# First attention layer in two groups of heads, with its projections, softmax and output projection interleaved

## The reference, cut to what matters

```python
def mla_mixer(h, cos, sin, w_down, q_a_norm, kv_a_norm, w_uq, w_ukv, q_norm, k_norm, w_o):
    down = h @ w_down                                    # 384 + 256 + 64 columns
    c_q = rmsnorm(down[..., :384], q_a_norm)
    c_kv = rmsnorm(down[..., 384:640], kv_a_norm)
    k_rope = down[..., 640:]
    q = (c_q @ w_uq).reshape(1, 256, 8, 192)             # per head 128 plain + 64 rotary
    kv = (c_kv @ w_ukv).reshape(1, 256, 8, 256)          # per head 128 key + 128 value
    k_nope, v = kv[..., :128], kv[..., 128:]
    k = concatenate([k_nope, broadcast(k_rope)], -1)
    q, k = rmsnorm(q, q_norm), rmsnorm(k, k_norm)        # over the head's 192 columns
    # rotary embedding on the last 64 columns of q and of k
    for blk in range(2):                                 # 128 queries at a time
        scores = einsum('bqhd,bkhd->bhqk', q[:, blk], k[:, :end]) * 192 ** -0.5
        p = softmax(where(causal, scores, -inf))
        outs.append(einsum('bhqk,bkhd->bqhd', p, v[:, :end]))
    return o @ w_o                                       # 1024 x 1024
```

## Time and profile before

| | us |
|---|---|
| median of three runs | 1415.55 |
| lowest and highest of them | 1414.0 to 1416.23 |
| the profiled execution, its own time | 1413.8 |
| its span from first to last instruction | 1411.8 |
| PE, DVE, ACT busy in the span | 1323.1, 1049.4, 864.3 |

### The profile page before, as it was taken

How to read it: one execution, slowest core, us unless ns; L and a number is a source line. 1 busy time by engine, 2 the same in 40 slices (tenths; PEclk the granted TensorE clock), 3 DMA queues, 4 the chain that set the end, 5 groups by cost and what they waited for, 6 DMA issues and landing times.

```text
span 1411.8 us, 18829 instructions
## 1 busy us (share of the span) xinstructions
PE 1323.1 (94%) x6088; PEld 1080.8 (77%) x6088; DVE 1049.4 (74%) x1488; ACT 864.3 (61%) x1274; POOL 38.8 (3%) x54
## 2 busy tenths in 40 slices
PE   7999999997687899999999999999997985999998
PEld 5878888886566788888888888888886753888887
DVE  4576555565755799999999999999995846555554
ACT  4655444456533587878787887878784544454443
POOL 0000000000300000000000000000000211000000
PEclk9999999998887999999999999999998977999999
DMA  9645545554013397979898999889894400355540
GB/s 356 217 143 207 179 179 191 195 178 150 1 60 120 147 383 296 383 299 377 316 367 330 340 342 337 338 338 371 325 375 134 179 30 1 119 182 195 188 150 30
DMA packets 46121, 319.30 MB, mean 226 GB/s; under 512 B 5152, under 2 KB 6304, under 8 KB 7808
## 3 DMA queue, kind: packets, MB, share of 16 engines
q1 hardware_dynamic: 44288, 316.39, 59.7%
q10 hardware_dynamic: 1680, 2.10, 0.5%
q0 software_dynamic: 112, 0.26, 0.1%
HBM read 316.64 MB, written 2.10 MB: 226 GB/s over the span
## 4 chain that ended last, share of the span: by engine, by line
PE 84%; DVE 9%; issue 3%; ACT 3%; DMA 1%; DVEq 0%; POOL 0%; SPq 0%; ACTq 0%; POOLq 0%
PE bank L350 24%; PE bank L352 24%; PE bank L351 24%; PE bank L641 2%; PE bank L414 2%; DVE wl L1223 2%; DVE x L1637 1%; PE bank L744 1%; PE bank L386 1%; DMA fixed<-fixed_dram 1%; PE bank L660 1%; PE bank L661 1%; PE bank L765 1%; PE bank L581 0%; PE bank L803 0%
## 5 line engine op out<-in xcount | busy, mean ns | idle before, releaser
L1223 DVE TENSOR_TENSOR wl<-raw,wh 128x1024 fp32r<-128x1024 f32 x598 | 714.8, 1221 | 208.5 <-ACT wh L828 197.7
L828 ACT ACTIVATE wh<-raw 128x1024 fp32r<-128x1024 f32 x598 | 631.4, 1061 | 327.3 <-PE bank L352 320.6
L350 PE MATMUL bank<-wh,xth 128*128 128x512 f32 (+2 forms) x1170 | 464.1, 397 | 15.0 <-DVE wl L1223 4.7
L352 PE MATMUL bank<-wh,xtl 128*128 128x512 f32 (+2 forms) x1170 | 455.4, 389 | 0.0
L351 PE MATMUL bank<-wl,xth 128*128 128x512 f32 (+2 forms) x1170 | 455.1, 389 | 0.0
L350 PEld LDWEIGHTS bank<-wh,xth 128*128 128x128 f32 x1170 | 221.8, 190 | 61.2 <-issue 7.7
L352 PEld LDWEIGHTS bank<-wh,xtl 128*128 128x128 f32 x1170 | 221.4, 189 | 46.2
L351 PEld LDWEIGHTS bank<-wl,xth 128*128 128x128 f32 x1170 | 222.2, 190 | 42.3
L350 PE MATMUL bank<-wh,hth 128*128 128x512 f32 x456 | 178.5, 391 | 0.0
L352 PE MATMUL bank<-wh,htl 128*128 128x512 f32 x456 | 177.9, 390 | 0.0
L351 PE MATMUL bank<-wl,hth 128*128 128x512 f32 x456 | 177.4, 389 | 0.0
(11 more groups left out here) (281 smaller groups left out, 853.5 us busy)
## 6 DMA issues: line engine op xcount, KB each, us to landing
raw<-weights_dram SPq DMA_DIRECT2D x299, 1024.0 KB, 4.9
x<-x_dram SPq DMA_DIRECT2D x1, 1024.0 KB, 7.7
bias_scratch<-act ACTq DMA_DIRECT2D x1, 1024.0 KB, 15.7
wide<-bias_scratch ACTq DMA_DIRECT2D x8, 128.0 KB, 2.6
out_dram<-x SPq DMA_DIRECT2D x4, 256.0 KB, 2.1
fixed<-fixed_dram SPq DMA_DIRECT2D x1, 596.0 KB, 8.8
rows<-rows_dram POOLq DMA_DIRECT2D x1, 256.0 KB, 6.1
cols<-cols_dram SPq DMA_DIRECT2D x1, 73.0 KB, 8.5
```

The source lines that it names most:

```text
L350: mm(o, lh, wh[:, wi, sl], start=start, stop=False)
L352: return mm(o, ll, wh[:, wi, sl], start=False, stop=stop)
L828: A(wh[:, c % SPLIT, :], raw[:, (c // 2) % RAW, (c % 2) * UNIT:(c % 2 + 1) * UNIT], ACT.Copy).then_inc(hi_done, 1)
L1223: V.tensor_tensor(wl[:, c % SPLIT, :], raw[:, (c // 2) % RAW, (c % 2) * UNIT:(c % 2 + 1) * UNIT], f32(wh[:, c % SPLIT, :]), ALU.subtract). ...
```

## The change

The stage's weights are stored in another order: units `R0` (rotary columns of all queries), `KA`, `QA0`, `VA` (keys, queries, values of heads 0 to 3), `KB`, `QB0`, `VB` (the same of heads 4 to 7), and the output projection by pairs of heads (`WO_UNITS`). Three units that are half empty are split over 512 columns only (`HALVED`). The latent rows are turned before their norm is known, the first eight transposes between the two last products of the down projection; the norm's factors enter later as scalars. The masked maximum of a head is made in one DVE operation for each of the two query blocks (`row_max`, a tensor-tensor-reduce with an accumulator), in place of four operations. The values are scaled on their copy out of PSUM, the keys straight from PSUM.

The order on PE (`c` and unit names as above):

```diff
+            pe.wait_ge(sem("qkT_d"), 1)
+            turn_k_rope(0, bank[6])
+            pe.wait_ge(sem("qkT_a"), 3)
+            pe.wait_ge(sem("qkT_d"), 3)
+            scores(0)
+            scores(1)
+            pe.wait_ge(sem("v_c"), 2)
+            product(QB0, 0, (0, 1), WIDE, bank[2:4], 0, 2)
+            turn_p(0)
+            scores(2)
+            product(QB0 + 1, 0, (2,), WIDE, bank[2:4], 0, 2)
+            values(0)
+            turn_p(1)
+            scores(3)
+            pe.wait_ge(sem("k_ready"), 2)
+            kv_chunk(VB, bank[0:2])
+            values(1)
+            turn_p(2)
...
+            scores(4)
+            scores(5)
+            wo(0)
+            turn_p(4)
+            scores(6)
+            wo(1)
+            values(4)
+            turn_p(5)
+            scores(7)
+            wo(2)
+            values(5)
+            turn_p(6)
+            wo(3)
+            values(6)
+            turn_p(7)
+            wo(4)
+            values(7)
+            wo(5)
+            wo(6)
+            turn_half("ffn1", 0, 4)
+            wo(7)
```

On DVE:

```diff
+            def row_max(h):
+
+                b = h % 2
+                dv.wait_ge(sem("head_S"), h + 1)
+                if h >= 2:
+                    dv.wait_ge(sem("head_PT"), h - 1)
+                for qb, (a, n) in enumerate(((0, P), (P, 2 * P))):
+                    c = 8 * (h // 4) + 4 * qb + h % 4
+                    r = V.tensor_tensor_reduce(out=ebuf[:, b, a:a + n], in0=bank[4 + b][:, a:a + n], in1=maskt[:, a:a + n],
+                                               scale=rs[:, c:c + 1], scalar=3.0e38, op0=ALU.add, op1=ALU.min,
+                                               accum_out=stat[:, 2 * b + qb:2 * b + qb + 1])
...
+            follow(KB, 1, 0)
+            q_scales(0)
+            evac_turned(4, 2048, bank[5], "kn")
+            evac_turned(6, 5120, bank[6])
+            row_max(0)
             k_sums(1)
...
+            follow(QB0, 1, 0)
+            row_max(1)
+            weigh(0)
+            k_scaled(1, bank[0:2])
+            follow(QB0 + 1, 1, 0)
+            row_max(2)
+            weigh(1)
+            out_lo(0)
+            q_sums(1)
+            follow(VB, 1, 0)
+            row_max(3)
+            weigh(2)
+            out_lo(1)
...
+            row_max(4)
+            row_max(5)
+            weigh(4)
+            follow(U_WO, 1, 0)
+            row_max(6)
+            out_lo(4)
+            follow(U_WO + 1, 1, 0)
+            weigh(5)
+            row_max(7)
+            out_lo(5)
+            follow(U_WO + 2, 1, 0)
+            weigh(6)
+            follow(U_WO + 3, 1, 0)
+            out_lo(6)
+            weigh(7)
+            out_lo(7)
+            follow(U_WO + 4, 1, 0)
```

On ACT in the output projection:

```diff
+            exps(4)
+            exps(5)
+            copy_p(4)
+            follow(U_WO, 1, 0)
+            exps(6)
+            out_hi(4)
+            follow(U_WO + 1, 1, 0)
+            copy_p(5)
+            exps(7)
+            out_hi(5)
+            follow(U_WO + 2, 1, 0)
```

More of the change, by code:

```diff
@@ L63 @@
 U_UQ = U_DOWN + 6
-U_UKV = U_UQ + 6
-U_WO = U_UKV + 4
+U_WO = U_UQ + 10
 U_MOE = U_WO + 8
@@ L561, in _ @@
[L561 to L570, removed]
+            product(U_DOWN + 4, 0, range(0, 4), 192, (bank[5], bank[7]), 0, KD - 1)
@@ L583, in _ @@
+            turn_q(1, 1, bank[0])
+            turn_k(1, 0, bank[1])
+            pe.wait_ge(sem("qkT_a"), 4)
+            turn_k(1, 1, bank[2])
+            pe.wait_ge(sem("qkT_d"), 4)
+            turn_k_rope(1, bank[3])
+            values(3)
             pe.wait_ge(sem("qkT_a"), 6)
             pe.wait_ge(sem("qkT_d"), 6)
[L585 to L612, removed]
-                        .then_inc(sem("head_O"), 1)
@@ L1005, in scale_q, with evac_q @@
-            def scale_q(heads):
-                for h in heads:
-                    for t in range(NT):
-                        A(qv[:, t, h, 0:NOPE], qv[:, t, h, 0:NOPE], ACT.Copy, scale=rs[:, 8 * t + h:8 * t + h + 1])\
-                            .then_inc(sem("q_ready"), 1)
-            for n in range(7):
-                if n < 3:
-                    follow(U_UQ + 2 * n, 2, 0)
+            def evac_q(half, banks):
+                for t in range(NT):
+                    A(act[:, t, 512 * half:512 * (half + 1)], banks[t][:, :], ACT.Copy).then_inc(sem("qn_c"), 1)
@@ new lines, in evac_v, with evac_turned @@
+            def evac_v(half, banks):
+                sc.wait_ge(sem("lora_rs"), 1)
+                for t in range(NT):
+                    A(act[:, t, 2560 + 512 * half:2560 + 512 * (half + 1)], banks[t][:, :], ACT.Copy,
+                      scale=rs[:, 50 + t:51 + t]).then_inc(sem("v_c"), 1)
+            def evac_turned(lot, at, o, gain=None):
+                sc.wait_ge(sem("qk_T"), lot)
+                g = {"scale": col(gain)} if gain else {}
+                A(wide[:, at:at + WIDE], o[:, :], ACT.Copy, **g).then_inc(sem("qkT_a"), 1)
@@ new lines, in out_hi @@
+            def out_hi(h):
+                sc.wait_ge(sem("head_O"), h + 1)
+                A(xth[:, oslot(h), :], bank[7][:, (h % 2) * 256:(h % 2 + 1) * 256], ACT.Copy).then_inc(sem("head_oh"), 1)
+            follow(R0, 2, 0)
+            for t in range(NT):
+                A(act[:, t, 1024:1536], bank[4 + 2 * t][:, :], ACT.Copy).then_inc(sem("r_c"), 1)
+            for t in range(NT):
+                sc.wait_ge(sem("r_c"), t + 1)
+                A(xn[:, t, 0:512], act[:, t, 1024:1536], ACT.Square).then_inc(sem("q_sq"), 1)
```

526 lines of the change are left out of this document (326 added, 200 removed).

## The result

The changed kernel takes 1429.02 us (median of 4, 1427.9 to 1430.4) against 1415.52 of before in the same comparison: ratio 1.0097, interval 1.008 to 1.0115. It is 13.5 us slower, where 5.0 was forecast, and lies above the range of 1409 to 1427.5. One single run in this document, of 5254 us in "A wide product directly behind a wait", is a slow one and is left out of the median and the ratio there.

The account below looks back on a forecast made before the run. PE was taken as the bound, busy 1323 of 1411.8 us. Waits of -5.4 - 1.6 - 3.6 + 14.7 + .9 = +5.0 and a clock term of 0, put on the median 1415.55, gave 1420.5 us, range 1409 to 1427.5.

Parts of the forecast that it names:

- A: Latent turn: the norm's chain leaves the path, so PE waits 2.2 us where it waited 7.6: -5.4 us.
- B: Projections: first chunks go to other banks, so PE's 1.6 us wait on ACT's copies goes: -1.6 us.
- C: Turning of the first group's queries and keys: PE waits 6 us on DVE where it waited 9.7: -3.6 us.
- D: Heads: division stands behind weight splits in the DVE and ACT queues; waits 22.5 us against 7.8: +14.7 us.
- E: First half's turn_half, right behind wo(6), waits for DVE's additions of the first chain: +.9 us.
- rival 3: Heads: DVE and ACT run far enough ahead that waits stay within 7.8 us; 1405.9 us, chance .10.
- F: PE's clock behind waits: six of eight returns at 1.7 us lose 10.2 us, against 10.0 before: 0.
- Rival 2: PE's clock falls at each wait: eight returns at 1.7 us, 13.6, add +3.6 us; 1424.1 us, chance .22.

Follow-up runs that it names:

- A wide product directly behind a wait: The changed kernel with the QB0 product moved from behind the first two heads' scores to directly behind the wait for the turned keys: 1422.22 us, ratio 1.0048.

## Why the prediction was wrong

**The waits, A to E: right in sum and nearly in each place.** Forecast +5.0, measured +3.0. A: 2.2 forecast, 1.83 measured. B: gone, as said. C: 6.1 forecast, and .96 + 3.73 + 1.57 = 6.3 measured, the two longer ones in the named places. D: 22.5 forecast, and 18.9 + 1.4 + 1.3 = 21.6 measured; heads 0 to 7 waited 3.8, 2.5, 3.1, 0, 0, 3.3, 3.3 and 2.8. `turn_p(3)` itself did not wait, the 1.4 came at `values(2)` ahead of it. E: no wait stands between `wo(6)` and `wo(7)`; the .9 was not there. `row_max` takes .75 from its first pass's start to the end of its last read, against .83 taken. Heads waiting no longer than before (rival 3) was wrong: they waited 21.6 against 7.8.

**The clock, F: the step that failed.** It said "At 1.7 us for each return, six of eight give 10.2, against 10.0 before: 0", with +3.6 as its upper bound. Measured is +12.5. The number of falls was nearly right, seven. The price of a return was half of the measured one: seven stretches lost 23.2, 3.3 each. The 1.7 came from one 4 us window behind the latent turn, whose stretch was longer than that window and had already begun in the wait. The profile before had the right price: finer windows of it show that its 10.0 us of loss (10.6 by half microseconds) stood in three stretches, 3.3 to 3.5 each, and I compared a total taken over whole stretches (10.0) with a count times a part of one (1.7). Six times 3.3 is 20, less 10.0 and with the waits' 5.0 gives 1430.5, near the measured 1429.0; some luck is in that, since the waits came out 2 lower and the falls one more. When a fall comes was not settled either: the text has it that the clock held at a pause of about 1, but in the heads before the change it fell at 403.64, right behind the third wait of .97 us in a row. Rival 2 had the mechanism and the same wrong price.

The second half of the error is what the runs added. The earlier trace rows had a window with 20 transposes, PE busy for 4.00 us, at .50. I read it as part of a stretch with waits; it also says that a busy PE does not by itself bring the clock back at once: the last wait ended at 370.40, and the clock came back at 376.34. The change put float32 scores behind four of its long waits, where the kernel before had wide products or transposes, and the product behind the keys' wait instead of the scores took that stretch from 5.7 to 2.5. How much of the seven stretches is due to this and how much to their number alone is not measured.

**A reading beside it.** "What is outside runs at 97 to 100%" does not hold for the 44 us behind the frame: PE works 31.84 us of them at .73 before, and 32.14 at .69 after. The forecast took nothing from there, and the 2 us by which the clock loss differs there come and go between the profiles, so the sum isn't touched; but a clock term was there too.

## What to carry to other kernels

In an in-order queue the work that is ready goes ahead of the work that waits for the consumer: moving the maxima and divisions ahead of the next weight split turned a change of +13.5 us into one of -12. Price a wait of TensorE with the whole low-clock stretch behind it, averaged over stretches (here 3.3 us for waits of 1.4 to 3.8), and not with one window, and keep a few microseconds of range, since the same wait brings a fall in one execution and none in another. Where a wait can't be removed, fill it, or put wide products directly behind it rather than float32 scores. The second shortened the stretch in both orders tried, and the total in one of the two: in the other, new waits took the gain back.

## What the runs showed of the hardware

- Fillers of 128 x 128 float32, 190 records in 22 us, held the granted clock at 1.00 over 111 us, where the same order without them had lost 23.2 us.
- Holding a full clock and bringing back a half one are not the same: scores of the same shape ran at 1.00 where no wait stood directly ahead and the clock was up, and stayed at .50 for 7.5 and 11.2 us of gapless work behind one. At the turned keys, a run of 512-column products brought the clock back 4.3 and 4.7 us after its start where only four transposes stood between it and the wait, and 2.9 to 5.3 us after its start where scores stood ahead of it. Narrow float32 work also ended a stretch: in the changed kernel PE made values and transposes of 128 columns without a gap from 391.76, and the clock was back at 397.91. So width alone is not the whole rule; what it is stays open.

```profile
391.76 0.77 PE L626 MATMUL bank<-hbuf,act 128*128 128x128 f32 x2 [1.36 <-DVE xtl L1729]
...
393.19 0.90 PE L617 MATMUL bank<-fixed,ebuf 128*128 128x128 f32 x3
...
396.44 1.06 PE L579 MATMUL bank<-fixed,xn 128*128 128x128 f32 x4
...
398.04 0.39 PE L628 MATMUL bank<-hbuf,act 128*128 128x128 f32 x2
```

- A float32 matmul of 128 columns is two records of .118 us each at full clock; x4 in a row of the timeline may be two instructions.
